# Two means of squares as two single-pass products each: one core, a two-layer hybrid encoder

## The chip, the cores and the metric

The kernel runs on one core of a Trainium2 chip. The metric is the device time of one execution in microseconds (us); three runs of the kernel before gave 1296.06, 1296.12 and 1297.22 us, so its median is 1296.12 us. Engines are called PE (TensorE), DVE (VectorE), ACT (ScalarE) and POOL (GpSimd); PEld is PE's weight load.

## The reference

Each of two layers normalises x (512 x 1024, fp32), projects it, runs three token mixers and merges them through sigmoid gates. What matters here is that the outputs of the first two mixers are each normalised over the 128 channels of a head:

```
def rms_norm(x, g):
    xf = x.astype(jnp.float32)
    y = xf * lax.rsqrt(jnp.mean(xf * xf, axis=-1, keepdims=True) + NORM_EPS)
    return (y * g.astype(jnp.float32)).astype(x.dtype)
...
    o_a = rms_norm(o_a.transpose(0, 2, 1, 3), gla_norm_g).reshape(B, S, BRANCH_W).astype(x.dtype)
    y_a = o_a * jax.nn.silu(a_g)
...
    o_b = rms_norm(o_b.transpose(0, 2, 1, 3), diff_norm_g) * (1.0 - lam_init)
    y_b = o_b.reshape(B, S, BRANCH_W).astype(x.dtype) * jax.nn.silu(b_g)
...
    mixed = jnp.sum(gates * z, axis=2)
    return x + jnp.einsum('bsd,de->bse', mixed, w_out)
```

There are four heads for each of the two mixers, two layers, and so 16 such means.

## The kernel before

Data lie transposed: channels on the 128 partitions, the 512 tokens along the free dimension. Each engine runs one hand-written program, and semaphores order them. Loops: layer L (2), and inside it group i (4), one head of the first mixer, one of the second and two of the third. So there are 8 groups, about 125 us apart within a layer.

The large projections are made in three passes with operands that are split into a rounded part and a low part in the type fp32r (`wh`, `wl` of the weights, `hh`, `hl` of the activations): wh·hh, wh·hl, wl·hh, each with PE in one pass. POOL makes `wh` (L380) and `wl` (two halves, L385) of every weight tile. Products of two plain fp32 operands are done by PE in several passes.

PE's order in the second part of a group is written out by hand. `scores(p)` (L1033, L1034) makes two score banks; DVE takes their row maxima (`row_max`, L794 or L800), ACT takes the exponential (`exp`, L601), DVE scales to weights (`weights(u)`, L829 to L834, last instruction L834 for u below 4, L841 from u = 4 on), and PE transposes them (`turn_weights(u)`, L1041), which waits for `w_ready`. Between these stand `fill(n)`: n steps of three projection passes (L927), work that covers the latency of the chain. ACT copies each transposed bank out (`turned(u)`, L609).

The first mixer's output stands in the bank `obank` (L1063) at u = 0. ACT squares it into `sqa` (L622), and DVE, which waits for that square, multiplies the bank by its gate into y (L850), and at u = 1, after a fill(5), PE multiplies `sqa` by the matrix `mean` (all 1/128, fp32) into `mbank` (L1072) and goes on with `turn_weights(1)`. The second mixer's output stands in `obank` at u = 4 (L1049): ACT squares it into `sqb` (L632), DVE gates it (L856) after weights(4), and PE makes the mean at u = 5 (L1084), after `turn_weights(5)`. ACT takes both reciprocal roots at u = 5, DVE applies them at u = 8 (L864, L865).

On POOL, two subtractions `low_parts` of 64 x 1024 elements (L318) for the third mixer's queries and keys stand between two weight tiles; in each group they run while DVE does the gating at u = 0 and the weights of u = 1. The tile `group` and the tile `yl` share memory, `qhat` and `kend` are slots 8 and 9 of it.

Of the kernel before, what the change touches and what calls it, by code (L numbers as in the profile page):

```python
# [15 lines left out]
F32 = mybir.dt.float32  # L16
F32R = mybir.dt.float32r
U32 = mybir.dt.uint32
ACT = mybir.ActivationFunctionType
ALU = mybir.AluOpType  # L20
AX_X = mybir.AxisListType.X

P = 128
DEPTH, S, D = 2, 512, 1024
KT = D // P
# [7 lines left out]
THETA, EPS = 10000.0, 1e-6  # L33
# [81 lines left out]
def sq_slot(e):  # L115

    return 0 if e == 0 else 1 + (e - 1) % 5
# [27 lines left out]
def build(nc, x_d, w_d, par_d, up_d, fin_d, cos_d, sin_d, lmask_d, cmask_d, gmask_d, ident_d, out_d, gate_d, xkeep_d):  # L145
    with ExitStack() as ctx:
        def sb(name, shape, dt=F32):
            return ctx.enter_context(nc.sbuf_tensor(name, shape, dt))
# [4 lines left out]
        def sig(name, per, credit=0):  # L153
            return Signal(ctx.enter_context(nc.semaphore(name)), per, credit)
# [19 lines left out]
        yl = sb("yl", [P, 3 * NG, S], F32R)  # L174
# [8 lines left out]
        rx, attsum = rr[:, 0, :], rr[:, 1, :]  # L183
        junk = rr[:, 1, 0:HD]
        sqa, sqb = rest, cum
        low = sb("low", [2 * RANK, S])
        total = sb("total", [P, NC])
        decay = sb("decay", [P, NC])
        att = sb("att", [P, 2, S])
        state = sb("state", [P, NC, DV])  # L190
# [4 lines left out]
        six = sb("six", [P, 6, S])  # L195
# [12 lines left out]
        cmask = sb("cmask", [P, S])  # L208
        gmask = sb("gmask", [P, 2, P], U32)
        ident = sb("ident", [P, P])  # L210
        mean = sb("mean", [P, P])
        cst = sb("cst", [P, 2])
        fin = sb("fin", [P, KT])

# [3 lines left out]
        obank, mbank = bank("obank"), bank("mbank")  # L218
# [8 lines left out]
        s_init = sig("s_init", 0)  # L227
# [3 lines left out]
        xsum_done = sig("xsum_done", 2)  # L231
# [6 lines left out]
        out_done = sig("out_done", 5)  # L238
# [15 lines left out]
        exp_done = sig("exp_done", 16)  # L254
        wt_ready = sig("wt_ready", 12, 1)
        sq_done = sig("sq_done", 2)
        r_done = sig("r_done", 1)
        act_grp = sig("act_grp", 4)

# [12 lines left out]
        max_ready = sig("max_ready", 16)  # L272
        w_ready = sig("w_ready", 12)
        y_read = sig("y_read", 3, 1)
        dve_grp = sig("dve_grp", 35)
        ab_normed = sig("ab_normed", 1)
        yl_ready = sig("yl_ready", 3 * NG)
# [171 lines left out]
        def _(act):  # L449
# [27 lines left out]
            with act.Fori(0, DEPTH) as L:  # L477
# [15 lines left out]
                with act.Fori(0, NG) as i:  # L493
                    G = L * NG + i
# [109 lines left out]
                    def turned(u):  # L604
                        act.wait_ge(*turn_done.at(G, u + 1))
                        if u == 4:
                            act.wait_ge(*out_done.at(G, 3))
                        q = (u if u < 4 else (u - 4) // 2) * P
                        act.activation((wt if u < 4 or u % 2 == 0 else wt1)[:, :, q:q + P], turn[u % 2][:, :].rearrange("p (k q) -> p k q", k=QB),  # L609
                                       ACT.Copy).then_inc(wt_ready.sem, 1)  # L610
# [5 lines left out]
                    for u in range(4):  # L616
                        exp(2 * u + 2)
                        exp(2 * u + 3)
                        if u == 0:
                            high_parts(1)  # L620
                            act.wait_ge(*out_done.at(G, 1))
                            act.activation(sqa[:, :], obank[:, :], ACT.Square).then_inc(sq_done.sem, 1)  # L622
                        turned(u)
                        if u == 0:
                            copy_high(1)
                            tanh_gate(2, "cg")
                        if u == 1:
                            copy_low(1)
                        if u >= 2:
                            merge_gate(u - 2)  # L630
                    act.wait_ge(*out_done.at(G, 3))
                    act.activation(sqb[:, :], obank[:, :], ACT.Square).then_inc(sq_done.sem, 1)  # L632
                    for u in range(4, 10):
                        exp(u + 6)
                        turned(u)
                        if u == 5:
                            merge_gate(2)

                            act.wait_ge(*out_done.at(G, 2))
                            grp.did(act.activation(rr[:, 0, :], mbank[:, :], ACT.Ln, bias=cst[:, 0:1]))  # L640
                            act.wait_ge(*out_done.at(G, 4))
                            grp.did(act.activation(rr[:, 1, :], obank[:, :], ACT.Ln, bias=cst[:, 0:1]))
                            grp.last()
                            act.activation(rr[:, :, :], rr[:, :, :], ACT.Exp, scale=-0.5).then_inc(r_done.sem, 1)
                        if u == 7:
                            merge_gate(3)
                        if u == 9:
                            merge_gate(4)
# [22 lines left out]
        def _(dve):  # L671
# [1 line left out]
            dve.sem_inc(z_read.sem, 6)  # L673
            dve.sem_inc(x_ready.sem, 8)
            dve.sem_inc(mixed.sem, 2)
            for t, val in ((mean[:, :], 1 / P), (cst[:, 0:1], EPS), (cst[:, 1:2], 1.0),
                           (state[:, :, :], 0.0), (att[:, :, :], 0.0)):
                last = dve.memset(t, val)
            last.then_inc(s_init.sem, 1)
            dve.wait_ge(*s_init.at(0, 1))  # L680

            def add_square(n, e):
                dve.wait_ge(*xsq_done.at(n, e + 1))
# [10 lines left out]
            with dve.Fori(0, DEPTH) as L:  # L694
# [33 lines left out]
                with dve.Fori(0, NG) as i:  # L728
                    G = L * NG + i
# [114 lines left out]
                    for u in range(4):  # L844
                        row_max(2 * u + 2)
                        row_max(2 * u + 3)
                        weights(u)
                        if u == 0:
                            dve.wait_ge(*sq_done.at(G, 1))
                            dve.scalar_tensor_tensor(y[:, i, :], obank[:, :], sc[:, 3:4], sg[:, 0, :], ALU.mult, ALU.mult).then_inc(y_read.sem, 1)  # L850
                        if u == 1:
                            silu(2, "cg")
                    row_max(10)
                    weights(4)
                    dve.wait_ge(*sq_done.at(G, 2))
                    dve.scalar_tensor_tensor(y[:, NG + i, :], obank[:, :], sc[:, 4:5], sg[:, 1, :], ALU.mult, ALU.mult).then_inc(y_read.sem, 1)  # L856
                    for u in range(5, 12):
                        if u < 10:
# [52 lines left out]
        @block.tensor  # L911
        def _(pe):
            pe.sem_inc(tile_done.sem, LAYER_TILES)
            pe.wait_ge(*s_init.at(0, 1))

            def x_mean(n):

                pe.wait_ge(*xacc_done.at(n, KT - 2))
                pe.matmul(mbank[:, :], mean[:, :], six[:, sq_slot(0), :], start=True, stop=False).then_inc(xsum_done.sem, 1)
                pe.wait_ge(*xsq_done.at(n, KT))  # L920
                pe.matmul(mbank[:, :], mean[:, :], six[:, sq_slot(KT - 1), :], start=False, stop=True).then_inc(xsum_done.sem, 1)

            def product(dst, slot, ks):

# [7 lines left out]
            with pe.Fori(0, DEPTH) as L:  # L932
# [14 lines left out]
                with pe.Fori(0, NG) as i:  # L947
# [69 lines left out]
                    def scores(p):  # L1017

                        if p == 0:
                            pe.wait_ge(*copied[0].at(G, 64))  # L1020
                            pe.wait_ge(*att_ready.at(G, 1))
                        elif p < 5:
                            pe.wait_ge(*exp_done.at(G, 2 * p))
                        else:
                            pe.wait_ge(*max_ready.at(G, 2 * p))
                        if p == 4:
                            pe.wait_ge(*copied[1].at(G, 64))
                        n, b = p // 4, p % 4
                        q = slice(P * b, P * b + P)


                        for head in range(2):
                            pe.matmul(score[head][:, :], yh[:, q_of(n, head), q], yh[:, high_of(n, head), :], start=True, stop=False)  # L1033
                            pe.matmul(score[head][:, :], yh[:, q_of(n, head), q], yh[:, low_of(n, head), :], start=False, stop=True).then_inc(score_done.sem, 1)  # L1034
# [9 lines left out]
                    def values(ready, done, *products):  # L1044
# [4 lines left out]
                                last = pe.matmul(dst, v[:, k, cols], weights[:, k, :], start=(k == 0), stop=(k == QB - 1))  # L1049
                        last.then_inc(done.sem, 1)  # L1050

                    scores(0)
                    fill(4)
                    scores(1)
# [12 lines left out]
                    for u in range(1, 4):  # L1067
                        scores(u + 1)
                        fill(5)
                        if u == 1:  # L1070
                            pe.wait_ge(*sq_done.at(G, 1))
                            pe.matmul(mbank[:, :], mean[:, :], sqa[:, :], start=True, stop=True).then_inc(out_done.sem, 1)  # L1072
                        turn_weights(u)
                    fill(3)
                    values(4, out_done, (obank[:, :], slice(P, 2 * P), wt))
                    for u in range(4, 10):
                        if u % 2 == 0:
                            scores(u // 2 + 3)
                        fill(3 if u in (5, 7) else 4)
                        turn_weights(u)  # L1080
                        if u == 5:
                            pe.wait_ge(*sq_done.at(G, 2))
                            pe.wait_ge(*y_read.at(G, 2))
                            pe.matmul(obank[:, :], mean[:, :], sqb[:, :], start=True, stop=True).then_inc(out_done.sem, 1)  # L1084
                    fill(4)
                    turn_weights(10)
                    turn_weights(11)
# [154 lines left out]
```

## Time and profile before

| | |
|---|---|
| median of 3 runs | 1296.12 us |
| profiled execution, its time | 1297.32 us |
| its span | 1295.3 us |
| mean granted TensorE clock | 0.99 |
| PE busy | 1232.5 us (95% of the span) |
| PEld busy | 983.1 us (76%) |
| POOL busy | 826.0 us (64%) |
| DVE busy | 649.4 us (50%) |
| ACT busy | 421.5 us (33%) |

The span runs from the first to the last instruction of the program. Matmuls overlap in their records, so the time that one takes from PE is read from the distance between two starts, not from its duration. Matmuls that stand in one row with x2 are two records of one product.

### The profile page before, as it was taken

The numbers are of one execution on the slowest core, as the hardware profiler recorded it, in microseconds if no ns is written. First come the engines' busy times: TensorE is split into PE (matmuls) and PEld (weight loads), VectorE is DVE, ScalarE is ACT, GpSimd is POOL, SyncE is SP. The second block draws the span as 40 slices with busy tenths as digits, with TensorE's granted clock in tenths as the row PEclk, the third lists the DMA queues.
The fourth block names the chain that finished last, engine by engine and source line by source line (L and its number), as shares of the span: only waits on it lengthen the run. The fifth ranks groups of instructions, "written<-read, shape, count | busy, mean of one in ns | idle before, by whom it ended". The sixth has DMA issues, their size and how long they took to land.

```text
span 1295.3 us, 18600 instructions
## 1 busy us (share of the span) xinstructions
PE 1232.5 (95%) x5836; PEld 983.1 (76%) x5836; DVE 649.4 (50%) x991; ACT 421.5 (33%) x753; POOL 826.0 (64%) x602
## 2 busy tenths in 40 slices
PE   3999999999999999999979999999999999999996
PEld 1887788778777877788858778877887788777884
DVE  6247335632653275577343743374247414837753
ACT  3414532443245234300142344145323532450001
POOL 6478547845774676578847763875288537866880
PEclk8999999999999999999989999999999999999999
DMA  7153314331342324374233332333243224234621
GB/s 292 36 147 98 117 49 130 113 115 52 110 132 97 95 85 134 107 259 163 86 134 98 102 103 90 113 96 105 76 142 85 99 81 146 89 114 173 240 82 65
DMA packets 51927, 150.59 MB, mean 116 GB/s; under 512 B 6576, under 2 KB 8112, under 8 KB 51376
## 3 DMA queue, kind: packets, MB, share of 16 engines
q1 hardware_dynamic: 29376, 106.72, 24.5%
q10 hardware_dynamic: 22512, 43.40, 10.9%
q8 instruction: 18, 0.29, 0.1%
q14 instruction: 21, 0.17, 0.0%
HBM read 114.45 MB, written 18.87 MB: 103 GB/s over the span
## 4 chain that ended last, share of the span: by engine, by line
PE 69%; DVE 11%; issue 8%; DMA 4%; POOL 3%; ACTq 2%; ACT 2%; DVEq 0%; POOLq 0%
PE proj L927 35%; PE proj L985 11%; DMA big<-big 4%; PE turn L1108 3%; PE turn L1041 3%; PE score L1108 3%; DVE w L834 3%; PE mbank L1049 2%; PE obank L1049 2%; ACTq L569 2%; PE mbank L1108 2%; PE obank L1108 2%; POOL big L408 1%; PE score L1034 1%; PE score L1033 1%
## 5 line engine op out<-in xcount | busy, mean ns | idle before, releaser
L385 POOL TENSOR_TENSOR wl<-raw_w,wh 128x512 fp32r<-128x512 f32 x356 | 497.2, 1417 | 33.3 <-POOL wh L380 33.3
L380 POOL TENSOR_SCALAR wh<-raw_w 128x1024 fp32r<-128x1024 f32 x178 | 210.4, 1182 | 326.5 <-PE proj L927 143.0
L927 PE MATMUL proj<-hh,wh 128*128 128x512 f32 x1024 | 406.8, 397 | 8.5 <-POOL wl L385 8.1
L927 PE MATMUL proj<-hh,wl 128*128 128x512 f32 x1024 | 400.2, 391 | 0.0
L927 PE MATMUL proj<-hl,wh 128*128 128x512 f32 x1024 | 399.4, 390 | 0.0
L927 PEld LDWEIGHTS proj<-hh,wh 128*128 128x128 f32 x1024 | 192.3, 188 | 51.8 <-issue 12.6
L927 PEld LDWEIGHTS proj<-hh,wl 128*128 128x128 f32 x1024 | 192.2, 188 | 41.8
L927 PEld LDWEIGHTS proj<-hl,wh 128*128 128x128 f32 x1024 | 192.5, 188 | 38.5
L800 DVE CUSTOM_DVE_ANT_0 six<-score,lmask 128x512 f32<-128x512 f32 x64 | 43.3, 686 | 138.8 <-PE score L1034 138.8
L609 ACT ACTIVATE big<-turn 128x512 f32<-128x512 f32 x96 | 56.3, 595 | 118.5 <-PE turn L1041 118.5
L985 PE MATMUL proj<-wh,hh 128*128 128x384 f32 x256 | 87.2, 341 | 0.1
L760 DVE TENSOR_TENSOR group<-big,group 128x512 f32<-128x512 f32 x24 | 36.8, 1586 | 97.5 <-ACT big L531 97.5
L985 PE MATMUL proj<-wh,hl 128*128 128x384 f32 x256 | 85.6, 334 | 0.0
L985 PE MATMUL proj<-wl,hh 128*128 128x384 f32 x256 | 85.6, 334 | 0.0
L462 ACT ACTIVATE six<-big 128x512 f32<-128x512 f32 x24 | 14.4, 628 | 208.6 <-DVE big L901 208.5
L1041 PEld LDWEIGHTS turn<-ident,w 128*128 128x128 f32 x384 | 45.9, 142 | 27.9 <-DVE w L834 19.4
L1041 PE MATMUL turn<-ident,w 128*128 128x128 f32 x384 | 57.3, 275 | 9.2 <-DVE w L834 9.2
L601 ACT ACTIVATE six<-score,negmax 128x512 f32<-128x512 f32 x64 | 43.5, 685 | 55.4 <-DVE negmax L794 55.2
L1033 PE MATMUL score<-yh 128*128 128x512 f32 x128 | 59.8, 467 | 0.0
L407 POOL TENSOR_TENSOR big<-big,cos 128x1024 f32<-128x1024 f32 x8 | 20.1, 2507 | 61.7 <-DMA big<-big 61.7
L985 PEld LDWEIGHTS proj<-wh,hh 128*128 128x128 f32 x256 | 48.0, 188 | 11.7 <-ACT group L505 6.1
L765 DVE TENSOR_TENSOR big<-big,cos 128x1024 f32<-128x1024 f32 x8 | 14.8, 1846 | 79.1 <-DMA big<-big 79.1
(162 smaller groups left out, 1806.3 us busy)
## 6 DMA issues: line engine op xcount, KB each, us to landing
raw_w<-weights SPq DMA_DIRECT2D x178, 512.0 KB, 3.3
gate_scratch<-gstage ACTq DMA_DIRECT2D x48, 256.0 KB, 2.0
six<-gate_scratch ACTq DMA_DIRECT2D x16, 768.0 KB, 5.0
big<-big ACTq DMA_DIRECT2D x64, 128.0 KB, 3.5
yh<-yh ACTq DMA_DIRECT2D x64, 128.0 KB, 3.1
x_scratch<-big SPq DMA_DIRECT2D x2, 2048.0 KB, 8.4
big<-x_scratch SPq DMA_DIRECT2D x2, 2048.0 KB, 10.1
big<-x_t SPq DMA_DIRECT2D x4, 512.0 KB, 5.9
```

The source lines that it names most:

```text
L380: pool.tensor_scalar(wh[:, slot, :, :], src, 1.0, 1.0, ALU.mult, ALU.mult).then_inc(pool_high.sem, 1)
L385: ins = pool.tensor_tensor(wl[:, slot, half, :], src[:, half, :], wh[:, slot, half, :].bitcast(F32), ALU.subtract)
L601: act.activation(probs[:, j % 4, :], src, ACT.Exp, bias=negmax[:, j:j + 1], scale=k, accum_out=sums[:, j:j + 1]).then_inc(exp_done.sem, 1)
L609: act.activation((wt if u < 4 or u % 2 == 0 else wt1)[:, :, q:q + P], turn[u % 2][:, :].rearrange("p (k q) -> p k q", k=QB), ACT.Copy).the ...
L800: dve.tensor_tensor_reduce(sneg[:, j % 2, :], score[j % 2][:, :], lmask[:, S - P - P * b:2 * S - P - P * b], -1.0, 3.0e38, ALU.add, ALU.mi ...
L834: dve.scalar_tensor_tensor(w[:, u % 2, :], probs[:, c % 4, :], rs[:, c:c + 1], w[:, u % 2, :], ALU.mult, ALU.add).then_inc(w_ready.sem, 1)
L927: last = pe.matmul(dst, a[:, slot, k, :], b[:, k, :], start=(k == 0 and a is wh and b is hh), stop=(k == KT - 1 and a is wl))
L985: last = pe.matmul(proj[b % 2][:, 0:3 * P], a[:, k, P * b:P * b + P], c[:, 0:3, k, :], start=(k == 0 and n == 0), stop=(k == KT - 1 and n ...
L1033: pe.matmul(score[head][:, :], yh[:, q_of(n, head), q], yh[:, high_of(n, head), :], start=True, stop=False)
L1041: last = pe.transpose(turn[u % 2][:, P * k:P * k + P], w[:, u % 2, P * k:P * k + P], ident[:, :])
L1049: last = pe.matmul(dst, v[:, k, cols], weights[:, k, :], start=(k == 0), stop=(k == QB - 1))
L1108: last = pe.matmul(zbanks[zt % 6][:, :], a[:, SLOT[c % BRANCH_SLOTS], n, :], (yl if is_low else yh)[:, b, :], start=(k == 0 and a is wh an ...
```

## The change

For both means, ACT squares the bank twice: once into the fp32 tile as before, and once into `sq_high`, an fp32r tile, which rounds. DVE subtracts the second from the first into `sq_low`, also fp32r. PE multiplies `mean`, now an fp32r tile, by `sq_high` and then by `sq_low`, both into the same bank. `sq_high` and `sq_low` are slots 8 and 9 of `yl`. The mean over x (twice two products, and once more at the end) keeps its fp32 form. `mean` can't be set directly in its new type: DVE fills a part of `att`, copies it over, and clears `att` after that.

```
+        sq_high, sq_low = yl[:, 8, :], yl[:, 9, :]
...
-        mean = sb("mean", [P, P])
+        mean = sb("mean", [P, P], F32R)
...
# ACT, u = 0
                             act.activation(sqa[:, :], obank[:, :], ACT.Square).then_inc(sq_done.sem, 1)
+                            act.activation(sq_high, obank[:, :], ACT.Square).then_inc(sq_high_done.sem, 1)
                         turned(u)
...
# ACT, ahead of u = 4
                     act.activation(sqb[:, :], obank[:, :], ACT.Square).then_inc(sq_done.sem, 1)
+                    act.wait_ge(*out_done.at(G, 2))
+                    act.activation(sq_high, obank[:, :], ACT.Square).then_inc(sq_high_done.sem, 1)
...
# DVE, start
-            for t, val in ((mean[:, :], 1 / P), (cst[:, 0:1], EPS), (cst[:, 1:2], 1.0),
-                           (state[:, :, :], 0.0), (att[:, :, :], 0.0)):
+            for t, val in ((att[:, 0, 0:P], 1 / P), (cst[:, 0:1], EPS), (cst[:, 1:2], 1.0),
+                           (state[:, :, :], 0.0)):
...
+            dve.tensor_copy(mean[:, :], att[:, 0, 0:P]).then_inc(s_mean.sem, 1)
+            dve.wait_ge(*s_mean.at(0, 1))
+            dve.memset(att[:, :, :], 0.0).then_inc(s_mean.sem, 1)
+            dve.wait_ge(*s_mean.at(0, 2))
...
# DVE, u = 0, and in the same form with sqb after weights(4)
                             dve.wait_ge(*sq_done.at(G, 1))
+                            dve.wait_ge(*sq_high_done.at(G, 1))
+                            dve.tensor_tensor(sq_low, sqa[:, :], sq_high.bitcast(F32), ALU.subtract).then_inc(sq_low_done.sem, 1)
                             dve.scalar_tensor_tensor(y[:, i, :], obank[:, :], sc[:, 3:4], sg[:, 0, :], ALU.mult, ALU.mult).then_inc(y_read.sem, 1)
...
# PE, u = 1, and with obank and 2 at u = 5 (there after the wait for y_read)
+                    def mean_of(dst, n):
+                        pe.wait_ge(*sq_high_done.at(G, n))
+                        pe.matmul(dst[:, :], mean[:, :], sq_high, start=True, stop=False)
+                        pe.wait_ge(*sq_low_done.at(G, n))
+                        pe.matmul(dst[:, :], mean[:, :], sq_low, start=False, stop=True).then_inc(out_done.sem, 1)
...
-                            pe.wait_ge(*sq_done.at(G, 1))
-                            pe.matmul(mbank[:, :], mean[:, :], sqa[:, :], start=True, stop=True).then_inc(out_done.sem, 1)
+                            mean_of(mbank, 1)
```

## Rows read from the trace of the kernel before

**Rows 1.** Busy time by engine, and the chain that ended last by engine

```profile
PE 1232.5 (95%) x5836; PEld 983.1 (76%) x5836; DVE 649.4 (50%) x991; ACT 421.5 (33%) x753; POOL 826.0 (64%) x602
...
PE 69%; DVE 11%; issue 8%; DMA 4%; POOL 3%; ACTq 2%; ACT 2%; DVEq 0%; POOLq 0%
```

**Rows 2.** Timeline of PE, second mean of group 0: start, duration, idle before

```profile
138.58 1.02 PE L1084 MATMUL obank<-group,mean 128*128 128x512 f32 x2
...
139.67 0.39 PE L1034 MATMUL score<-yh 128*128 128x512 f32 x1
139.90 0.39 PE L1033 MATMUL score<-yh 128*128 128x512 f32 x1
```

**Rows 3.** Timeline of PE, group 1: mean and turn at u = 1, turn 5

```profile
238.79 1.02 PE L1072 MATMUL mbank<-group,mean 128*128 128x512 f32 x2
240.45 0.66 PE L1041 MATMUL turn<-ident,w 128*128 128x128 f32 x4 [0.64 <-DVE w L834]
...
262.83 0.60 PE L1041 MATMUL turn<-ident,w 128*128 128x128 f32 x4
```

**Rows 4.** Timeline of DVE, group 1, from the gating of y to weights(3)

```profile
234.95 0.75 DVE L850 SCALAR_TENSOR_TENSOR y<-obank,sc,group 128x512 f32 x1 [1.43 <-ACT group L622]
...
237.65 2.75 DVE L834 SCALAR_TENSOR_TENSOR w<-six,rs,w 128x512 f32<-128x512 f32 x1
240.32 0.68 DVE L777 SCALAR_TENSOR_TENSOR group<-group,proj 128x512 f32<-128x512 f32 x1
...
249.22 0.75 DVE L834 SCALAR_TENSOR_TENSOR w<-six,rs,w 128x512 f32<-128x512 f32 x1
```

**Rows 5.** Timeline of POOL, group 1, the same stretch

```profile
234.84 2.40 POOL L318 TENSOR_TENSOR yh<-big,yh 64x1024 fp32r<-64x1024 f32 x1 [0.18 <-POOL wl L385]
237.41 2.44 POOL L318 TENSOR_TENSOR yh<-big,yh 64x1024 fp32r<-64x1024 f32 x1 [0.18 <-POOL yh L318]
240.29 1.05 POOL L380 TENSOR_SCALAR wh<-raw_w 128x1024 fp32r<-128x1024 f32 x1 [0.44 <-POOL yh L318]
```

**Rows 6.** Timeline of ACT, group 1, at both squares

```profile
234.19 0.60 ACT L622 ACTIVATE group<-obank 128x512 f32<-128x512 f32 x1 [0.28 <-PE obank L1063]
234.69 0.59 ACT L609 ACTIVATE big<-turn 128x512 f32<-128x512 f32 x1
...
256.83 0.60 ACT L632 ACTIVATE group<-obank 128x512 f32<-128x512 f32 x1 [4.43 <-PE obank L1049]
258.20 0.73 ACT L601 ACTIVATE six<-six,negmax 128x512 f32<-128x512 f32 x1 [0.77 <-DVE negmax L800]
```

**Rows 7.** Timeline of DVE, group 7: weights(0) and weights(1)

```profile
1113.39 1.64 DVE L834 SCALAR_TENSOR_TENSOR w<-six,rs,w 128x512 f32<-128x512 f32 x1
...
1120.18 1.61 DVE L834 SCALAR_TENSOR_TENSOR w<-six,rs,w 128x512 f32<-128x512 f32 x1
```

**Rows 8.** Timeline of POOL, group 7, the same stretch

```profile
1114.66 2.62 POOL L318 TENSOR_TENSOR yh<-big,yh 64x1024 fp32r<-64x1024 f32 x1 [0.18 <-POOL wl L385]
1117.46 2.40 POOL L318 TENSOR_TENSOR yh<-big,yh 64x1024 fp32r<-64x1024 f32 x1 [0.18 <-POOL yh L318]
1120.21 1.05 POOL L380 TENSOR_SCALAR wh<-raw_w 128x1024 fp32r<-128x1024 f32 x1 [0.35 <-POOL yh L318]
```

**Rows 9.** Timeline of DVE, group 4: a sum of two SBUF tiles

```profile
725.10 0.69 DVE L789 TENSOR_TENSOR group<-att 128x512 f32<-128x512 f32 x1
```

**Rows 10.** Timeline of POOL, group 4, beside it

```profile
725.20 2.86 POOL L407 TENSOR_TENSOR big<-big,cos 128x1024 f32<-128x1024 f32 x1 [7.87 <-DMA big<-big]
```

**Rows 11.** Timeline of DVE, group 1, around the second gating, then weights(5)

```profile
258.28 0.51 DVE L841 TENSOR_SCALAR w<-six,rs 128x512 f32<-128x512 f32 x1
258.71 0.74 DVE L856 SCALAR_TENSOR_TENSOR y<-obank,sc,group 128x512 f32 x1
...
260.17 0.48 DVE L841 TENSOR_SCALAR w<-six,rs 128x512 f32<-128x512 f32 x1
```

**Rows 12.** Timeline of POOL, group 1, behind the second gating

```profile
261.80 1.06 POOL L380 TENSOR_SCALAR wh<-raw_w 128x1024 fp32r<-128x1024 f32 x1 [3.30 <-PE proj L927]
```

More of the change, by code:

```diff
@@ L256, in build @@
         sq_done = sig("sq_done", 2)
+        sq_high_done = sig("sq_high_done", 2)
         r_done = sig("r_done", 1)
@@ L274, in build @@
         y_read = sig("y_read", 3, 1)
+        sq_low_done = sig("sq_low_done", 2)
+        s_mean = sig("s_mean", 0)
         dve_grp = sig("dve_grp", 35)
@@ L855, in _ @@
                     dve.wait_ge(*sq_done.at(G, 2))
+                    dve.wait_ge(*sq_high_done.at(G, 2))
+                    dve.tensor_tensor(sq_low, sqb[:, :], sq_high.bitcast(F32), ALU.subtract).then_inc(sq_low_done.sem, 1)
                     dve.scalar_tensor_tensor(y[:, NG + i, :], obank[:, :], sc[:, 4:5], sg[:, 1, :], ALU.mult, ALU.mult).then_inc(y_read.sem, 1)
@@ L913, in _ @@
             pe.sem_inc(tile_done.sem, LAYER_TILES)
-            pe.wait_ge(*s_init.at(0, 1))
+            pe.wait_ge(*s_mean.at(0, 1))
             def x_mean(n):
                 pe.wait_ge(*xacc_done.at(n, KT - 2))
-                pe.matmul(mbank[:, :], mean[:, :], six[:, sq_slot(0), :], start=True, stop=False).then_inc(xsum_done.sem, 1)
+                pe.matmul(mbank[:, :], mean[:, :].bitcast(F32), six[:, sq_slot(0), :], start=True, stop=False).then_inc(xsum_done.sem, 1)
                 pe.wait_ge(*xsq_done.at(n, KT))
-                pe.matmul(mbank[:, :], mean[:, :], six[:, sq_slot(KT - 1), :], start=False, stop=True).then_inc(xsum_done.sem, 1)
+                pe.matmul(mbank[:, :], mean[:, :].bitcast(F32), six[:, sq_slot(KT - 1), :], start=False, stop=True).then_inc(xsum_done.sem, 1)
             def product(dst, slot, ks):
@@ L1081, in _ @@
                         if u == 5:
-                            pe.wait_ge(*sq_done.at(G, 2))
                             pe.wait_ge(*y_read.at(G, 2))
-                            pe.matmul(obank[:, :], mean[:, :], sqb[:, :], start=True, stop=True).then_inc(out_done.sem, 1)
+                            mean_of(obank, 2)
                     fill(4)
```

## The prediction

> **What bounds the kernel now.** I read the busy table and the chain of waits first: PE is busy in 95% of the span and holds 69% of the chain that ended last, and DVE with 11% is next [rows 1]. So work taken from PE counts, unless PE waits right behind it; and work added on DVE counts where PE waits for DVE. I therefore read the timelines at the two means, engine by engine. The groups repeat the pattern of group 1 closely, so that one is priced and the odd ones are set apart.
>
> At u = 1, PE starts the mean at 238.79 and turn_weights(1) at 240.45; the row says 0.64 us idle, released by weights(1) on DVE (L834), and that one ends at 240.40 [rows 3, 4]. So this mean stands in front of a wait for DVE. At u = 5 it stands behind turn 5, and projections or scores follow it at once [rows 2]: there PE's time is real.
>
> **What a mean costs PE.** From 138.58 to 139.67 are 1.09 us, for two records of the mean and one score pass. A single pass is 0.23 (139.67 to 139.90), so the mean holds PE for 1.09 - 0.23 = 0.86 us [rows 2]. Two single-pass products hold it for 2 x 0.23 = 0.46. The change frees 0.40 us per mean. At u = 5 that is won in each of 8 groups: 8 x 0.40 = 3.2 us. At u = 1 PE only waits 0.40 us longer for DVE: nothing is won.
>
> **What is added on ACT.** A second square, 0.60 long, started 0.50 behind the first, as L609 does now (234.19, 234.69) [rows 6]. At u = 0 the rounded square ends at 235.29, and everything behind it on ACT (turned(0), the issues of copy_high, the tanh of cg, exp(4)) moves by 0.5; exp(4) then waits for its row maximum anyway, which below comes 2.75 us later. At u = 4 it ends near 257.9, before exp(10) starts at 258.20 [rows 6]: free. Its wait for the first mean is long fulfilled.
>
> **What is added on DVE, u = 4.** The subtraction has two SBUF inputs of 128x512; the same form takes 0.69 alone [rows 9]. It starts where the gating stood, 258.71, POOL being idle for the 3.30 us up to 261.80 [rows 11, 12]. Behind it row_max(11) and weights(5) move by 0.69: weights(5) ends at 260.65 + 0.69 = 261.34, turn 5 starts at 262.83 [rows 3, 11], 0.4 us earlier at most once PE is faster, so 1.1 us of cover is left. If that cover were gone, it would cost up to the 0.69. I take 0. POOL waits for PE in this stretch.
>
> **What is added on DVE, u = 0: the term that decides.** DVE now waits for the rounded square (235.29, some 0.16 later it can start, as y does now behind the first: 234.79 to 234.95), subtracts, and only then gates y. Its two inputs meet POOL's L318. The rows show what happens then: weights(1) takes 2.75 us against 0.75 when POOL is idle, and ends at 240.40, 0.55 behind the end of the L318 beside it (237.41 + 2.44 = 239.85) [rows 4, 5]. DVE waited for POOL. The other way round, POOL waits: L407, started 0.10 behind a DVE sum that kept its 0.69, took 2.86 [rows 9, 10]; and L318 of group 7 ends 2.25 behind the end of DVE's weights(0) (1115.03, 1117.28) [rows 7, 8]. In the Trainium skill, "SBUF — State Buffer", section "Who interferes with whom", this is an exclusive lock: a DVE instruction with two SBUF inputs and a GpSimd instruction that reads SBUF block each other, and the first to issue goes first. The trace agrees (2.75 against 0.75 us), and the rule speaks against this change, which puts such an instruction in front of DVE's critical chain.
>
> For group 1 that gives, in steps:
> 1. The subtraction is ready at 235.45, after L318 began (234.84). It ends 0.55 behind L318's end: 237.24 + 0.55 = 237.79.
> 2. y starts 0.08 earlier than that end, as L777 does behind a delayed L834 (240.32 against 240.40) [rows 4]: 237.71, where before it was 234.95: 2.76 later. From y's start to L834's start are 2.70 (237.65 - 234.95): the new L834 starts at 240.41.
> 3. The second L318 lets the subtraction pass and ends 2.25 behind it: 240.04. POOL's L380 follows 0.44 behind [rows 5]: 240.48.
> 4. So L834 now misses the second L318, on which it lost 2.0 us before, and starts 0.07 ahead of L380. If it gets through it takes 0.75 and ends at 241.16, 0.76 later than before. If L380 (1.05) gets in first, L834 ends 0.55 behind it: 242.08, 1.68 later.
>
> Which one? DVE's start 0.10 ahead was enough once [rows 9, 10]; in group 7, with this very pair, 0.03 ahead (1120.18, 1120.21) was not: L834 took 1.61 [rows 7, 8]. 0.07 lies between, a little nearer to the case that got through. I take 0.76 and keep 1.68 for the range.
>
> Two groups are apart, since POOL's code for the last group of a layer is written out and its L380 follows in 0.35 instead of 0.44 [rows 8]. There L380 starts 0.02 ahead of L834, which loses: in group 3 the new end is 0.35 - 0.44 = 0.09 before the 1.68 case, +1.6. Group 7 had lost that race before: by the same steps L380 starts at 1117.28 + 0.55 + 2.25 + 0.35 = 1120.43 and L834 ends at 1120.43 + 1.05 + 0.55 = 1122.03, against 1121.79: +0.2.
>
> Does PE pay it in full? It waits for weights(1) already, so turn 1 moves by as much, and scores(3), row_max(6), weights(2), for which it waits too, start from it. POOL's L380 moves with L834 (it ends some 0.9 behind it), so the meetings of weights(2) with POOL move as a whole. I see no slack afterwards that takes it back: the later waits start from PE's own events.
>
> **The start.** DVE's copy and waits come while PE waits for x; a few tenths of a us there have cover of many. The mean of x keeps its form. 0.
>
> **The sum.** u = 0/1: 6 x 0.76 + 1.6 + 0.2 = +6.4. u = 5: -3.2. Together +3.2 us: on the profiled execution 1297.32 + 3.2 = 1300.5; that execution lies 1.2 above the median of the runs, so on the median 1296.12 + 3.2 = 1299.3 us.
>
> **Rivals.**
> - *L380 gets in first in all groups.* 6 x 1.68 + 1.6 + 0.2 = 11.9, less 3.2: +8.7, 1304.8 us. For it: the lost race of group 7 by 0.03 [rows 7, 8]. Against: 0.07 is over twice that lead. Chance 0.27.
> - *The subtraction is not held up by the first L318* (ends the other way). It would end at 235.45 + 0.69 = 236.14; L834 would start at 236.14 - 0.08 + 2.70 = 238.76, still beside the second L318, and end at 240.40 as before. The 2.0 us that L834 loses there now would hide the 1.1 us added, PE would win 3.2: 1292.9 us. It decides at a delay of 2.0 us. Against: it needs two SBUF inputs to run beside L318, which L834 did not [rows 4, 5]. Chance 0.08.
> - *The late weights are partly absorbed*, or PE wins nothing at u = 5 because the two waits inside the mean cost as much: somewhere from 1296.1 to 1302.5 (6.4 without the 3.2). Chance 0.1.
> - The forecast: 0.55.
>
> **Range and chances.** The forecast's own range is 1298.0 to 1300.5: the terms of 0.76 hang on starts read to 0.05 us, and there are eight groups. With the second case the range is 1297.2 to 1305.5, which leaves out the faster rival and the ends of the others. A difference under 0.2% (2.6 us, edges 1293.5 and 1298.7) is about what a measurement of this kernel can't tell from none. The forecast lies 0.6 above that edge, so about 0.38 of its 0.55 counts as slower, and 0.17 as the same. With 0.27 and some 0.04 of the third: slower 0.68; same 0.24; faster 0.08.
>
> **What the profile after would show.** The subtraction at u = 0 at 2.3 us, ended 0.55 behind the first L318; L834 of u = 1 at 0.75 us in six groups (or 1.7 in all); PE's wait for weights(1) at about 1.8 us instead of 0.64, for the mean now takes 0.46; at u = 5 two records with starts 0.23 apart, no new wait behind; ACT's exp(10) unmoved. The prediction is wrong if the subtraction runs in 0.69 beside L318, if L834's race with L380 falls the other way, or if the wait for weights(1) shrinks again in a later step, as in POOL's weights.

## The result, and the profile after

The changed kernel takes 1303.08 us in the median of 6 runs (1301.48 to 1305.51); the kernel before took 1296.09 us beside it (1295.49 to 1297.77, 6 runs). The ratio is 1.0052, 95% interval 1.004 to 1.0064: slower by about 0.5%. The profiled executions have spans of 1301.1 and 1295.3 us, 5.8 us apart. The runs of the changed kernel spread over 4.0 us, those of before over 2.3.

In the new file turn_weights stands at L1056, the two products of a mean at L1069 and L1071, weights(u) at L840 to L845 (L852 from u = 4 on), the first subtraction and gating at L862 and L863, the second at L870 and L871, POOL's `low_parts` at L322 and its weight tiles at L384 and L389. The page of the changed kernel, busy time and the chain that ended last:

```profile
PE 1231.1 (95%) x5836; PEld 987.0 (76%) x5836; DVE 661.9 (51%) x1008; ACT 429.4 (33%) x769; POOL 830.1 (64%) x602
...
PE 67%; DVE 9%; issue 9%; DMA 5%; POOL 4%; ACTq 3%; ACT 2%; DVEq 0%; POOLq 0%
```

DVE has 12.5 us more work and ACT 7.9 us. The change is not in these sums but in a wait. PE's waits in the changed kernel, line waited for, us in total, times, longest:

```profile
PE turn L1056 <- DVE w L845: 18.0, 13, 2.7
```

The timeline of DVE in group 1 of the changed kernel, to be held against [rows 4]:

```profile
235.56 2.44 DVE L862 TENSOR_TENSOR yl<-group,yl 128x512 fp32r<-128x512 f32 x1 [1.83 <-ACT yl L627]
237.92 0.74 DVE L863 SCALAR_TENSOR_TENSOR y<-obank,sc,group 128x512 f32 x1
...
240.09 0.48 DVE L843 TENSOR_SCALAR w<-six,rs 128x512 f32<-128x512 f32 x1
240.60 0.75 DVE L845 SCALAR_TENSOR_TENSOR w<-six,rs,w 128x512 f32<-128x512 f32 x1
```

POOL in the same stretch, against [rows 5]:

```profile
235.04 2.40 POOL L322 TENSOR_TENSOR yh<-big,yh 64x1024 fp32r<-64x1024 f32 x1 [0.18 <-POOL wl L389]
237.62 2.61 POOL L322 TENSOR_TENSOR yh<-big,yh 64x1024 fp32r<-64x1024 f32 x1 [0.18 <-POOL yh L322]
240.67 1.59 POOL L384 TENSOR_SCALAR wh<-raw_w 128x1024 fp32r<-128x1024 f32 x1 [0.44 <-POOL yh L322]
```

And PE, against [rows 3]:

```profile
238.98 0.39 PE L1069 MATMUL mbank<-yl,mean 128*128 128x512 f32 x1
239.22 0.39 PE L1071 MATMUL mbank<-yl,mean 128*128 128x512 f32 x1
241.41 0.66 PE L1056 MATMUL turn<-ident,w 128*128 128x128 f32 x4 [1.80 <-DVE w L845]
```

The subtraction takes 2.44 us and ends at 238.00, 0.56 behind the end of the first L322 (237.44). The gating follows, L845 starts 0.07 ahead of POOL's L384, gets through in 0.75, and POOL's instruction is the one that is held (1.59 instead of 1.05). Turn 1 waits 1.80 us where it waited 0.64. All of this is as forecast, the lead of 0.07 included. In groups 3 and 7 L384 starts 0.01 to 0.02 ahead of L845, which then takes 1.56.

The second mean, PE in group 1 of the changed kernel, against [rows 2]:

```profile
264.14 0.47 PE L1069 MATMUL obank<-yl,mean 128*128 128x512 f32 x1
264.45 0.39 PE L1071 MATMUL obank<-yl,mean 128*128 128x512 f32 x1
264.69 0.39 PE L1048 MATMUL score<-yh 128*128 128x512 f32 x1
```

No wait stands in front of any of them, and turn 6 of every group comes 0.40 to 0.42 us earlier, relative to turn 5, than before. DVE there, against [rows 11]:

```profile
259.64 0.68 DVE L870 TENSOR_TENSOR yl<-group,yl 128x512 fp32r<-128x512 f32 x1
260.25 0.74 DVE L871 SCALAR_TENSOR_TENSOR y<-obank,sc,group 128x512 f32 x1
```

**What no step forecast.** In group 3 turn 1 is late by 1.56 us, as forecast, and turn 2 by a further 1.08, although it waits for nothing. PE's timeline there:

```profile
492.38 0.80 PE L1056 MATMUL turn<-ident,w 128*128 128x128 f32 x4 [2.60 <-DVE w L845]
492.83 0.78 PE L1048 MATMUL score<-yh 128*128 128x512 f32 x1
493.40 0.63 PE L1049 MATMUL score<-yh 128*128 128x512 f32 x1
493.83 0.63 PE L1048 MATMUL score<-yh 128*128 128x512 f32 x1
494.26 0.63 PE L1049 MATMUL score<-yh 128*128 128x512 f32 x1
```

A single pass now takes 0.43 us from start to start (493.83 to 494.26) instead of 0.23. Two windows of the changed kernel (stretch, length, busy us and instructions of PE, PEld, DVE, ACT, POOL, granted TensorE clock, DMA): the first lies in group 6 behind turn 1, the second in group 3 ahead of it.

```profile
1001.40:1004.70 3.30, 3.30 (x10) 2.52 (x9) 3.07 (x6) 1.66 (x5) 3.30 (x3) 0.50 0.35 79
490.00:492.30 2.30, 0.00 (x0) 0.00 (x0) 2.23 (x6) 0.90 (x4) 1.77 (x3) 1.00 0.00 0
```

The granted clock is 1.00 while PE stands idle, and 0.50, the lower of its two levels (1.2 GHz), behind that. It fell so in groups 3, 6 and 7, behind waits of 2.60, 1.89 and 2.69 us; the five other waits, of 1.77 to 1.89 us, saw no fall. Turn 2 is later by 1.08, 1.03 and 1.02 us in these three. The kernel before had no fall inside its groups. The mean granted clock of the whole span hides this: it is 0.990 before and 0.991 after, since the profile of before also has half clock from 19.6 to 33.3 us, near the start, which that of after has not. It cost nothing that shows: turn 0 of group 0 is 0.06 us apart in the two.

The profiled difference, turn by turn: turn 1 in the six ordinary groups 0.74 to 0.86 each, 4.7 together; group 3 1.6; group 7 0.6; the three falls 3.1; the second means -3.2. That is +6.8; turn 11 of the last group is +5.8 late. The missing -1.0 are steps of up to 0.3 us ahead of turn 0, which come out differently from group to group, and smaller ones behind; what sets them was not traced.

### The profile page after: what moved, and what is told of

Same layout as the page of the kernel before. It is cut to its first block, busy times and chain, and to the rows that moved or that the text cites. A ratio compares the mean times of both kernels' runs of the same rounds, so it can differ in the third digit from the quotient of the medians.

```text
span 1301.1 us, 18649 instructions
## 1 busy us (share of the span) xinstructions
PE 1231.1 (95%) x5836; PEld 987.0 (76%) x5836; DVE 661.9 (51%) x1008; ACT 429.4 (33%) x769; POOL 830.1 (64%) x602
## 4 chain that ended last, share of the span: by engine, by line
PE 67%; DVE 9%; issue 9%; DMA 5%; POOL 4%; ACTq 3%; ACT 2%; DVEq 0%; POOLq 0%
PE proj L942 34%; PE proj L1000 10%; DMA big<-big 5%; PE turn L1127 3%; PE turn L1056 3%; PE score L1127 3%; ACTq L573 2%; PE mbank L1064 2%; PE obank L1064 2%; POOL big L412 2%; PE mbank L1127 2%; PE obank L1127 2%; PE score L1049 1%; PE score L1048 1%; DVE big L777 1%
## 5 line engine op out<-in xcount | busy, mean ns | idle before, releaser
L389 POOL TENSOR_TENSOR wl<-raw_w,wh 128x512 fp32r<-128x512 f32 x356 | 497.3, 1417 | 33.2 <-POOL wh L384 33.2
L384 POOL TENSOR_SCALAR wh<-raw_w 128x1024 fp32r<-128x1024 f32 x178 | 213.2, 1198 | 328.7 <-PE proj L942 145.3
L1056 PE MATMUL turn<-ident,w 128*128 128x128 f32 x384 | 57.2, 275 | 18.0 <-DVE w L845 18.0
L1056 PEld LDWEIGHTS turn<-ident,w 128*128 128x128 f32 x384 | 46.2, 142 | 32.4 <-DVE w L845 23.5
L411 POOL TENSOR_TENSOR big<-big,cos 128x1024 f32<-128x1024 f32 x8 | 19.2, 2401 | 61.1 <-DMA big<-big 61.1
```

The lines of the kernel that those rows point to most:

```text
L384: pool.tensor_scalar(wh[:, slot, :, :], src, 1.0, 1.0, ALU.mult, ALU.mult).then_inc(pool_high.sem, 1)
L389: ins = pool.tensor_tensor(wl[:, slot, half, :], src[:, half, :], wh[:, slot, half, :].bitcast(F32), ALU.subtract)
L1056: last = pe.transpose(turn[u % 2][:, P * k:P * k + P], w[:, u % 2, P * k:P * k + P], ident[:, :])
```

## The experiments

All medians are to be held against the kernel before in the same comparison: 1296.41 us for "The second mean alone", "The first mean alone", "The subtraction with one SBUF input" and "More work in the wait"; 1296.11 for "Only the wait for the second square", "The subtraction behind the row maxima", "POOL waits behind its two subtractions" and "The second mean alone, with POOL giving way"; 1297.10 for "Giving way twice". "Late" and "early" of a turn are read from the profiles, against that of the kernel before, each turn measured from the one ahead of it. An ordinary group is any but 3 and 7.

**The second mean alone.**

```
# the first mean keeps its form of before:
+pe.wait_ge(*sq_done.at(G, 1))
+pe.matmul(mbank[:, :], mean[:, :].bitcast(F32), sqa[:, :], start=True, stop=True).then_inc(out_done.sem, 1)
-mean_of(mbank, 1)
# and at u = 0 neither the second square nor the subtraction
```

> Only the second mean (u = 5) is split; the first is the fp32 product of before. Theory A (the second mean wins 0.40 us per group, the first costs): 1296.1 - 8 x 0.40 = 1292.9 us, L845 of u = 1 blocked for 2.75 us as before, no fall of the clock inside the groups. Rival B (the waits inside a split mean eat its gain; the loss is spread over both means): 1296 to 1300 us.

Measured: 1292.99 us, ratio 0.9976 (0.9966 to 0.9986). Turn 6 is 0.40 to 0.42 earlier in each group, and no fall of the clock lies inside the groups. The weights at u = 1 are held for 2.75 us in seven groups, as expected. Theory A holds, B falls: this half of the change wins what its sum said.

**The first mean alone.**

```
-mean_of(obank, 2)
+pe.wait_ge(*sq_done.at(G, 2))
+pe.matmul(obank[:, :], mean[:, :].bitcast(F32), sqb[:, :], start=True, stop=True).then_inc(out_done.sem, 1)
# and at u = 4 neither the second square nor the subtraction
```

> Only the first mean (u = 1) is split; the second is the fp32 product of before. Theory A: weights(1) late by 0.7 to 0.8 us in six groups and by about 1.5 in groups 3 and 7, +6 us, and +1.0 us for each fall of TensorE's clock behind the longer wait (three in the profile of the changed kernel): 1302 to 1306 us, above the changed kernel by 3.2. Rival B: between 1296 and 1301 us.

Measured: 1305.87 us, ratio 1.0075 (1.006 to 1.0089), at the upper end of theory A. The two halves add up: -3.4 and +9.5 give +6.1, the changed kernel has +7.0. In the profile turn 1 is late by 0.57 to 0.75 us in five ordinary groups and by 1.69 and 1.37 in groups 3 and 7, where the clock falls. Two things were not expected. In group 6 turn 1 comes 0.30 earlier; there POOL's two subtractions begin 0.4 us ahead of turn 0 instead of 0.9 behind it. And 1.1 us is lost between the layers, where the clock is at half for 10.2 us instead of 6.8. So that the halves add up to within 1 us is in part chance.

**The subtraction with one SBUF input.**

```
-dve.tensor_tensor(sq_low, sqa[:, :], sq_high.bitcast(F32), ALU.subtract).then_inc(sq_low_done.sem, 1)
+dve.tensor_tensor(sq_low, obank[:, :], sq_high.bitcast(F32), ALU.max).then_inc(sq_low_done.sem, 1)
```

> The first subtraction is replaced by a maximum of the PSUM bank obank and sq_high, so that it has one SBUF input instead of two; the low part of the first mean is thereby not computed. Everything else is as in the changed kernel. Theory A (the subtraction's price is that POOL's subtraction of queries and keys holds it up): it takes 0.7 us instead of 2.5, L845 of weights(1) starts 1.1 us later than in the kernel before and still ends 0.55 behind POOL's second L322, as before; the first mean costs nothing, no fall of the clock, 1292.9 us. Rival C (the cost is the 1.1 us of added ACT and DVE work in DVE's chain, whatever POOL does): weights(1) is late by 0.8 us or more in each group, 1299 us or more.

Measured: 1299.01 us, ratio 1.0018 (1.0009 to 1.0026). This kernel leaves out the low part of the first mean, so only its time is of use. Theory A is right on the instruction and wrong on the result. DVE in group 1 of this run:

```profile
235.31 0.69 DVE L862 TENSOR_TENSOR yl<-obank,yl 128x512 fp32r<-128x512 f32 x1 [1.86 <-ACT yl L627]
...
238.09 1.92 DVE L843 TENSOR_SCALAR w<-six,rs 128x512 f32<-128x512 f32 x1
240.04 0.75 DVE L845 SCALAR_TENSOR_TENSOR w<-six,rs,w 128x512 f32<-128x512 f32 x1
```

POOL beside it:

```profile
234.76 2.40 POOL L322 TENSOR_TENSOR yh<-big,yh 64x1024 fp32r<-64x1024 f32 x1 [0.18 <-POOL wl L389]
237.34 2.38 POOL L322 TENSOR_TENSOR yh<-big,yh 64x1024 fp32r<-64x1024 f32 x1 [0.18 <-POOL yh L322]
```

The maximum runs in 0.69 beside POOL's L322 with one SBUF input (L322 from 234.76 to 237.16). But the 2.0 us that L834 lost in the kernel before [rows 4] are no cushion: L843, the scaling in front of it, has to wait for POOL's second subtraction as well (1.92 instead of 0.48, until 0.29 behind its end at 239.72). In the kernel before the same instruction (L832) started at 237.13, ahead of the second subtraction (237.41 [rows 5]), and so only L834 met it. The kernel before shows the other case too: in group 7 its L832 started behind the second subtraction (1117.46 [rows 8]) and was held.

```profile
237.13 0.48 DVE L832 TENSOR_SCALAR w<-six,rs 128x512 f32<-128x512 f32 x1
...
1117.77 2.38 DVE L832 TENSOR_SCALAR w<-six,rs 128x512 f32<-128x512 f32 x1
```

Either way weights(1) hangs on the end of POOL's second subtraction: it is done 0.55 us behind that end when L834 is the one held (240.40 against 239.85 [rows 4, 5]), and 1.07 behind it when L843 is (240.79 against 239.72 here). The step between the two is 0.5 us, for every delay that still puts L843 beside that subtraction.

In this run turn 1 is late by 0.4 to 0.7 us in the six ordinary groups and by 1.5 and 1.0 in groups 3 and 7, the two in which the clock falls. Rival C wanted 0.8 us or more in each group; its time (1299 or more) is met, its lateness is not. Theory A2 was formed here: what decides is on which side of POOL's second subtraction L843 falls, not how much DVE is late.

**Only the wait for the second square.**

```
 dve.wait_ge(*sq_high_done.at(G, 1))
-dve.tensor_tensor(sq_low, sqa[:, :], sq_high.bitcast(F32), ALU.subtract).then_inc(sq_low_done.sem, 1)
# and the first mean is the product with sq_high alone
```

> The changed kernel without the first subtraction and without the product of the first low part, so that the first mean is of the rounded squares alone; DVE still waits for the second square, 0.5 us. Theory A (cushion of 2.0 us): 1292.9 us, weights(1) on time. Theory A2: L843 starts 0.5 us later, behind the start of POOL's second subtraction, and is held for 2.4 us; weights(1) is late by about 0.55 us, with perhaps one to three falls of the clock: 1297 to 1300 us, about as much as with the PSUM input, though less is added.

Measured: 1298.22 us, ratio 1.002 (1.0011 to 1.0029). DVE in group 1:

```profile
235.47 0.75 DVE L862 SCALAR_TENSOR_TENSOR y<-obank,sc,group 128x512 f32 x1 [1.96 <-ACT yl L627]
...
237.66 2.40 DVE L843 TENSOR_SCALAR w<-six,rs 128x512 f32<-128x512 f32 x1
```

L843 is 0.5 us later than before and takes 2.40 us. Turn 1 is late by 0.37 to 0.47 us in five ordinary groups and by 0.28 and 0.94 in groups 3 and 7, with one fall of the clock (group 7). Half a microsecond of delay costs nearly what 1.1 us cost in the run before (+2.1 us against +2.6 on the kernel before): A2 holds, the cushion falls. Group 4 is an exception, and POOL differs there: its two subtractions begin 0.3 us ahead of turn 0 instead of 0.9 behind it, and turn 1 comes 0.55 earlier although L843 is held.

**The subtraction behind the row maxima.**

```
 row_max(2 * u + 3)
+if u == 1:
+    dve.wait_ge(*sq_high_done.at(G, 1))
+    dve.tensor_tensor(sq_low, sqa[:, :], sq_high.bitcast(F32), ALU.subtract).then_inc(sq_low_done.sem, 1)
 weights(u)
# and no longer in front of the gating, which still waits for the second square
```

> The changed kernel with the first subtraction moved behind row_max(5), in front of weights(1), instead of in front of the gating of y. Theory A as in the prediction (the price is DVE's delay beyond a cushion of 2.0 us): L845 of u = 1 starts at 238.5 in group 1's terms, still beside POOL's second subtraction, and ends 0.2 us later than before: about 1294.5 us. Theory A2, formed on the run with the PSUM input (what decides is whether the scaling L843 slips in between POOL's two subtractions; whatever delays it makes it wait for the second one, and L845 comes behind that): weights(1) is late by 0.7 us all the same, 1299.5 to 1303.5 us.

Measured: 1313.82 us, ratio 1.0136 (1.0121 to 1.0151): outside both. DVE in group 1:

```profile
241.43 0.68 DVE L860 TENSOR_TENSOR yl<-group,yl 128x512 fp32r<-128x512 f32 x1
...
242.35 2.28 DVE L843 TENSOR_SCALAR w<-six,rs 128x512 f32<-128x512 f32 x1
```

The subtraction slips in between POOL's two, and L843 is held for 2.28 us all the same, as A2 says. Turn 1 is 0.90 to 0.97 late in five ordinary groups, 1.1 in group 0, and 2.8 and 1.5 in groups 3 and 7; in group 3 the subtraction itself meets POOL's second one and takes 2.90. The profile has six stretches of half clock inside the groups, against three in the changed kernel, five of them behind turn 1, each with 1.0 to 1.4 us at turn 2. In group 0, PE also waits 2.3 us for POOL's `wl` at the fill ahead of u = 0 (1.0 in the changed kernel at most), with a fall behind it: POOL had waited 8.89 us for a DMA ahead of its L411 instead of 7.92, and stayed 1.0 us late. What held the DMA is open. Against the profile of the changed kernel this run is 7.6 us longer: turn 1 is 2.4 of it, the further falls at turn 2 are 2.5, group 0 is 2.6. But the profiled execution took 1310.56 us and the other three 1313.76 to 1313.96, so 3.3 us of the median stand in no profile.

**More work in the wait.**

```
 pe.wait_ge(*sq_high_done.at(G, n))
+if n == 1:
+    for _ in range(4):
+        pe.matmul(dst[:, :], mean[:, :], sq_high, start=True, stop=True)
```

> The changed kernel with four more single passes of mean by sq_high into the same bank ahead of the first mean; their results are overwritten. Theory A (part of the loss is TensorE's clock, which falls to half for a stretch behind the longer wait for weights(1)): the 0.92 us of work lies in that wait, which shrinks to about 0.85 us in six groups and 1.7 in groups 3 and 7; the falls inside the groups become fewer or go, each is worth 1.0 us, the time is 1299.5 to 1301.5 us and spreads less than 1301.5 to 1305.5. Rival D (the clock's falls are incidental): 1303 us or more, with as many falls.

Measured: 1299.73 us, ratio 1.0026 (1.0017 to 1.0036), 3.3 us faster than the changed kernel with 32 more products. PE in group 1 (L1071 x4 are the added products), and its total of this wait:

```profile
238.74 1.07 PE L1071 MATMUL mbank<-yl,mean 128*128 128x512 f32 x4
...
241.27 0.66 PE L1056 MATMUL turn<-ident,w 128*128 128x128 f32 x4 [1.01 <-DVE w L845]
```

```profile
PE turn L1056 <- DVE w L845: 11.7, 17, 1.6
```

The longest wait is 1.6 us, no stretch of half clock is left inside the groups, and the runs spread over 1.7 us instead of 4.0. Of the 3.7 us by which the last turns of the last group come earlier than in the changed kernel, the three falls at turn 2 are 3.1. The clock's share of the loss is thereby shown, some 3 of 7.0 us; rival D falls.

**POOL waits behind its two subtractions.**

```
 pool.wait_ge(*c_parts.at(G, 1))
+pool.wait_ge(*w_ready.at(G, 2))
```

> The changed kernel, but POOL waits for weights(1) before it goes on behind its two subtractions, so that L845 can't lose the port to L384. If the lost race is what makes groups 3 and 7 dearer: L845 takes 0.75 us in all 8 groups instead of 1.56 in those two, 1.6 us are won back, and the falls of the clock in them, 1.0 us each, become rarer, since the wait there is 0.8 us shorter: 1299.5 to 1301.5 us. If it is not: 1303 us.

Measured: 1295.9 us, ratio 1.0002 (0.9989 to 1.0016), with runs from 1294.76 to 1304.3; the profiled execution took 1301.04 us, with half clock inside the groups for 6.8 us in group 0 (behind a wait of 2.4 us for POOL, which again had a late DMA, 9.15 us instead of 7.92) and 3.4 us in group 6. The last instruction of weights(1) (L845, here L846) takes 0.75 us in all 8 groups, groups 3 and 7 included: the lost race is what made them dearer. The median lies 3.6 us below the lower end of what was expected, for POOL's tiles were shifted for u = 2 too: turn 2 comes 0.44 to 0.51 us earlier in seven groups (3.2 us), since L844 of weights(2) (L843 elsewhere) now takes 0.51 us where the kernel before had 1.20 (L832 at 243.14):

```profile
247.01 0.51 DVE L844 TENSOR_SCALAR w<-six,rs 128x512 f32<-128x512 f32 x1
247.56 1.66 DVE L846 SCALAR_TENSOR_TENSOR w<-six,rs,w 128x512 f32<-128x512 f32 x1
```

**The second mean alone, with POOL giving way.** The runs above point to POOL's second subtraction as what PE waits for in the kernel before too.

```
# on the kernel with the second mean alone
+pool.wait_ge(*w_ready.at(G, 2))
 low_parts(pool, raw, 1, 1).then_inc(c_parts.sem, 1)
```

> Only the second mean split, and POOL's second subtraction of queries and keys waits until weights(1) is done. If POOL's hold on the port at u = 1 is what PE waits for in the kernel before too, L845 of u = 1 takes 0.75 us, weights(1) is ready about 2.0 us earlier, PE's wait (0.75 us) goes in all groups, and 1293.0 falls by up to 8 x 0.75 to about 1287 us. Rival: the low parts come 1 us later and scores(4), which waits for their copies, takes back what was won: 1290 us or more.

Measured: 1289.43 us, ratio 0.995 (0.9937 to 0.9963). It lies between what was expected (about 1287) and the rival's 1290. Turn 1 gains 0.75 to 1.08 us in all groups and turn 2 some 0.5 in seven, where turn 3 gives 0.8 back. PE, DVE and POOL in group 1, at u = 1 and u = 3:

```profile
238.78 0.60 PE L1054 MATMUL turn<-ident,w 128*128 128x128 f32 x4
...
249.28 0.66 PE L1054 MATMUL turn<-ident,w 128*128 128x128 f32 x4 [0.65 <-DVE w L845]
```

```profile
246.50 1.02 DVE L843 TENSOR_SCALAR w<-six,rs 128x512 f32<-128x512 f32 x1
247.56 1.66 DVE L845 SCALAR_TENSOR_TENSOR w<-six,rs,w 128x512 f32<-128x512 f32 x1
```

```profile
245.94 2.73 POOL L389 TENSOR_TENSOR wl<-raw_w,wh 128x512 fp32r<-128x512 f32 x2 [0.18 <-POOL wh L384]
```

Turn 1 waits for nothing. The rival named the wrong wait (scores(4) is on time), but part is given back: POOL is later, and its next weight tile now stands beside weights(3).

**Giving way twice.**

```
# on the kernel of the run before
+if u == 3 + UNIT_TILES.index("m3"):
+    pool.wait_ge(*w_ready.at(G, 4))
```

> As the run in which only the second mean is split and POOL's second subtraction waits for weights(1), and POOL also waits for weights(3) before it splits the weight tile m3. There PE's wait moved from u = 1 to u = 3 (0.65 us, L843 and L845 held up by POOL's L389). If that is the same loss in another place: weights(3) takes 0.48 and 0.75 us, turn 3 comes 0.8 us earlier in each group, 1289.4 - 6.2 = 1283.2 us. Rival: POOL is then so late with m3 and its followers that PE waits for them, or the race moves on once more: 1287 us or more.

Measured: 1283.92 us, ratio 0.9896 (0.988 to 0.9913), 0.7 above the forecast of 1283.2. Turn 3 gives nothing back any more; in one group (4) turn 5 is 0.6 late. DVE at u = 3 in group 1, and what is left of PE's wait for the weights below u = 4:

```profile
246.38 0.48 DVE L845 TENSOR_SCALAR w<-six,rs 128x512 f32<-128x512 f32 x1
246.89 0.75 DVE L847 SCALAR_TENSOR_TENSOR w<-six,rs,w 128x512 f32<-128x512 f32 x1
```

```profile
PE turn L1056 <- DVE w L847: 1.5, 2, 0.8
```

This version beats both kernels, by 1.0% the one before.

## Why the prediction was right, and where it was not

- **The price of a mean on PE** (0.86 us, 0.46 after) and its place: right. The second mean won 0.40 per group, 3.2 us, and alone 3.4 us.
- **The first mean's PE time is worth nothing**: right. Turn 1 started when weights(1) was done.
- **The subtraction held by POOL's L318, and the new place of L834**: right step by step, 2.44 us, and 0.74 to 0.86 late per ordinary group against 0.76. The steps leave out L832 in front of L834, without harm here: its counterpart L843 started at 240.09, when the second L322 was 0.14 us from its end, and took its usual 0.48.
- **The race of L834 with L380**: right, in the six groups won by 0.07 us, in group 3 lost (+1.56 against +1.6). Group 7 cost 0.6 against 0.2: turn 1 is 1.4 later, measured from turn 0, but in the kernel before L832 of weights(0) had been held there too (1.57 us), turn 0 had waited 0.73 for it, and that wait is gone. The prediction placed 0.07 between two single cases. The profiles of all runs show 40 meetings of this pair at u = 1, started at most 0.12 us apart: ahead by 0.07 to 0.12 us the DVE instruction took 0.75 in all 28, and ahead by 0.03 or less, or behind by 0.02, it took 1.56 to 1.61 in all 12.
- **The terms taken as 0 behind u = 4**: right. exp(10) moved by 0.03 us apart from the lateness of its group (259.17 against 258.20 + 0.94), and no turn from 6 on waits.
- **Nothing taken back, nothing added later**: this is where the size went wrong. "Does PE pay it in full?" was answered by the waits behind turn 1 alone. What the longer wait does to PE's clock had no term: three falls of 1.0 us in the profile, and 3.3 us of the median between the changed kernel and the run with four more passes. With it the sum is +3.2 + 3.3 = +6.5 against +7.0 measured. The profile of before gave a hint of it in the 0.50 that it shows between the layers (658 to 664 us), and its waits inside the groups, at most 1.2 us, had shown no fall.
- **The faster rival** was priced at 1292.9 us by a cushion of 2.0 us that isn't there. Its working stepped over L832, the scaling in front of L834. Two runs showed it: with the subtraction freed from POOL 1299.01, with the subtraction gone 1298.22. The conclusion that the rival was unlikely stood on another reason and was not touched.
- **L380 first in all groups** (1304.8 us) came closer to the median than the forecast, but the profile shows that it did not happen: six groups won the race.

The time of 1303.08 lies outside the forecast's own range of 1298.0 to 1300.5. It lies in the stated range of 1297.2 to 1305.5 by luck: that range reached so far because of the first rival (L380 first in all groups), which did not happen, and not because of the clock, which did.

## What to carry to other kernels

A product in front of a wait is free on its engine: ask first what the wait is for, since work taken from the product wins nothing, while work added to that chain can cost (here 2.8 us at the gating became 0.8 at turn 1). When two engines share a port, a delay is not a sum of durations but a question of which instruction falls beside which; follow every instruction of the chain, the short ones too, past the other engine's, and consider letting the engine off the critical path wait on purpose. When a wait of PE grows, price the clock behind it as well as the wait.

## What was not expected of the hardware

The granted clock fell to 0.50 behind PE waits as short as 1.89 us in a stretch where PE was otherwise busy, and did not behind five others of 1.77 to 1.89; it cost 1.0 us each time. With the subtraction behind the row maxima it fell behind a wait of 1.99 us in group 1 and not behind one of 1.99 in group 2. So the length of the wait alone doesn't decide it here, and what does is open. Filling part of the wait with products that nobody reads made the kernel 3.3 us faster. DVE's TENSOR_SCALAR with one SBUF input (L843) took up to 2.44 us beside POOL's subtraction against 0.48 alone, while a TENSOR_TENSOR with one SBUF and one PSUM input ran beside the same POOL instruction in 0.69. The Trainium skill, "SBUF — State Buffer", section "Who interferes with whom", states both: a copy or tensor_scalar can run in a mode that takes both ports, and one SBUF input outside of it doesn't contend. The runs agree with both (2.40 and 0.69 us in group 1); that L843 ran in such a mode no record says.
